# Expert 0's tokens formed by products with strided columns of the token rows, in three parts

## The chip, the cores and the metric

The kernel runs on one core of a Trainium2 chip. The metric is the device time of one execution in microseconds (us). Engines are named as in the profile: PE (TensorE matmul), PEld (its weight loads), DVE (VectorE), ACT (ScalarE), POOL (GpSimd), SP (SyncE, which issues all the DMAs).

## What is computed

One decoder layer on 256 tokens of 1024 features, in float32. A token mixer comes first (gated DeltaNet, a short convolution and cross-attention, each projected, gated and summed, and then an output projection), followed by a residual and a LayerNorm. Then comes the expert part, which is where the change lies:

```
h = layer_norm(DEEPNORM_ALPHA * h + mix)
logits = h @ w_router + b_router             # 32 experts, each token takes its best 4
# for each expert e, over the tokens routed to it:
gate, up = split(x_e @ w_gate_up[e] + b_gate_up[e])         # 1024 -> 2 x 1024
hid = (clip(up, -7, 7) + 1) * min(gate, 7) * sigmoid(1.702 * min(gate, 7))
y_e = (hid @ w_down[e] + b_down[e]) * weight                # 1024 -> 1024
h = layer_norm(DEEPNORM_ALPHA * h + sum over experts of y_e)
```

The weights of one expert are 12 MB, and all 32 are read: this is nearly all of the 453 MB that the kernel moves.

## The kernel before

**The stages.** The mixer runs for the first quarter of the span, by a schedule made in `mixer_schedule` (L100); its products are three float32r products for one float32 product (`three`, L1287). Its last product is `wo`, in two column halves; the second runs from 305.7 to 317 us. Then come the router's logits (L1366), the choice of the four best experts (`top_four`, L1736), and the ranks of the tokens within their expert (schedule step `("rank", 0)`, PE at L1467). After that, 32 items follow, one for each expert. One item takes a block of up to 64 tokens.

**An item on PE.** `gate_up` (L1505) adds the bias by four small products with a one-hot row of the expert (`bias`, L1498), then runs four parts q = 0 to 3. Each part uses one 2 MB piece of weights (two 128-row slices of the 1024 features) against `x_slotT`, the item's tokens with features on partitions (`128x4x128`: four feature blocks, two column halves c of 64 slots). `down` (L1612) uses two more 2 MB pieces. Products with an output of 64 partitions are made in pairs on the two column halves of the array.

**How an item's tokens are made.** Before, in every item: PE gathers the rows by a one-hot product (`gather`, L1484, tokens on partitions), ACT copies them from PSUM to `x_tok` (`copy_rows`, L1235), PE turns four blocks of every fourth column (`turn_tokens`, L1492, columns `slice(b, 4 * P, 4)`, L349), and DVE applies the LayerNorm's gain and bias on the way to `x_slotT` (`copy_tokens`, L1988). For items 1 onward this happens one item ahead, behind the products. For item 0 it stands between the rank step and the first product with weights; `first_tokens` (L2015) does the DVE part in two halves, so that q = 0 waits for `half_tokens` and q = 1 for `tokens_in`.

**The residuals.** The old rows `hx`, scaled by ACT (`scaled_rows`, L1107), are turned back into four PSUM banks by `residual` (L1359), in the order `AGAIN` (L884). One of the four stands behind item 0's gather and the others behind q = 1, 2, 3.

**The ring of weights.** There are 12 places of 2 MB, two items' worth. Piece m goes to place m mod 12 (`ring_place`, L856), and the SP program issues its DMA when the piece that stood there is used (`chunk_spent`, L868): after q = 0, 1, 2 by the semaphore `chunks_used`, after q = 3 by `gu_done`, after the first half of `down` by `chunks_used`, and after the second by `down_done`. Pieces 0 to 5 are item 0's, 6 to 11 item 1's, and 12 is the first whose place item 0 must clear. The places of pieces 0 to 11 overlap what the mixer holds. Piece 2 waits for the mixer's last piece of weights to be split (L938). Pieces 7, 9 and 11 wait for the end of `wo` (L947); place 7 lies exactly over `act_hi` and `act_lo`, the input of `wo`.

**The order of work on PE around the change**, written out at L1659 to L1668: wait for the rank bank to be free, wait for `onehots`, gather, one residual, turn, `gate_up` of item 0, turn of the hidden rows, turn of item 1's tokens, `down`. In the `rank` step, PE turns old rows (`turn_again`, L1353) and then waits for the second mask (L1476).

Of the kernel before, what the change touches and what calls it, by code (L numbers as in the profile page):

```python
# [33 lines left out]
ALU = mybir.AluOpType  # L34
# [3 lines left out]
P = 128  # L38
# [134 lines left out]
def hybrid_layer(nc, x, mem, ln0_g, ln0_b, w_in, conv_qkv, conv_mix, a_log, dt_bias, gdn_norm,  # L173
                 w_mem_kv, w_br, w_o, ln1_g, ln1_b, w_router, b_router, w_gate_up, b_gate_up,
                 w_down, b_down, ln2_g, ln2_b, out):
    with ExitStack() as ctx:
# [147 lines left out]
        wr_o = scratch_o  # L324
        gwr = l.at(x1_o + 512, KD, NE)
        assert l.used >= x1_o + 1536

        def xT(t, k, n=1):

            o = (x1_o + 1024 + k * P if k < 4 else x1_o + (k - 4) * P) if t == 0 else scratch_o + 2 * (1024 - 128) - (KD - k) * P  # L330
            return l.at(o, n * P)
# [48 lines left out]
        bank_free = [sem(f"bank_free{n}") for n in range(BANKS)]  # L380
        bank_hi = sem("bank_hi")
        router_sums, router_row, gains_in = sem("router_sums"), sem("router_row"), sem("gains_in")
        ln1_rows, tokens_made = sem("ln1_rows"), sem("tokens_made")
        again, cut_rows = sem("again"), sem("cut_rows")
        counted, row_made, half_tokens = sem("counted"), sem("row_made"), sem("half_tokens")
        consts, pads = sem("consts"), sem("pads")
# [503 lines left out]
        def _(sp):  # L890
            def bcast(dst, src, done):
                sp.dma_start(dst, src).then_inc(done, 16)

            sp.dma_start(mem_tok, mem[0].rearrange("(t p) d -> p t d", p=P)).then_inc(mem_in, 16)
            slot_dma(sp, 0, 0)
# [41 lines left out]
            for c in range(RAW):  # L937
                raw_spent(sp, N_MIX - RAW + (c - N_MIX) % RAW)  # L938
                chunk_dma(sp, c, w_gate_up[0, 0], w_down[0, 0], *ring_place(c)[0:2])
                if c == 0:  # L940

                    sp.wait_ge(bank_full[bank_of(("br", 0, KD - 1))], turn_of(("br", 0, KD - 1)))
                    for m in BEHIND_BRANCHES:
                        if m == EC:
                            wait_sums(sp, KD)
                        chunk_dma(sp, m - EC, w_gate_up[0, 1], w_down[0, 1], *ring_place(m)[0:2])
            sp.wait_ge(bank_full[bank_of(("wo", 1, 1))], turn_of(("wo", 1, 1)))  # L947
            for m in range(EC, RING):
                if m != SPARE and m not in BEHIND_BRANCHES:
                    chunk_dma(sp, m - EC, w_gate_up[0, 1], w_down[0, 1], *ring_place(m)[0:2])  # L950
# [39 lines left out]
        def _(pool):  # L990
# [90 lines left out]
            eng.memset(ranks, NOT_HERE)  # L1081
            eng.memset(weights, 0.0)
            eng.memset(ids, 0.0).then_inc(moe_consts, 1)


        @block.scalar
        def _(act):
# [147 lines left out]
            def copy_rows(i):  # L1235
                act.wait_ge(gathered, i + 1)
                a.copy(x_tok, ps[0][:, :]).then_inc(rows_copied, 1)  # L1237
# [12 lines left out]

            copy_rows(0)
            for t in range(NT):
# [24 lines left out]
        def _(pe):  # L1277
# [88 lines left out]
            def logit_rows(t, ks):  # L1366
# [17 lines left out]
            for s in SCHEDULE:  # L1384
# [99 lines left out]
            def gather():  # L1484
# [5 lines left out]
                ins.then_inc(gathered, 1)  # L1490

            def turn_tokens(i):  # L1492
                pe.wait_ge(rows_copied, i + 1)
# [4 lines left out]
            def bias():  # L1498

                for c in range(2):  # L1500
                    for n in range(2):
                        rows = slice(NE * (2 * n + c), NE * (2 * n + c + 1))
                        mm(ps[1 + n][64 * c:64 * c + 64, :], e_row[rows, :], bgu[rows, :], start=True, stop=False)  # L1503

            def gate_up(i, places, first=False, tables=False, parts=None):  # L1505

                if first:
                    pe.wait_ge(row_made, 1)
                    pe.wait_ge(ebias_in, 128)
                else:  # L1510
                    pe.wait_ge(tokens_in, i + 1)
                bias()
# [98 lines left out]

            def down(i, places, parts=None, own_scatter=False):  # L1612
                pe.wait_ge(hid_copied, i + 1)
                for q in range(2):
# [43 lines left out]

            pe.wait_ge(bank_free[bank_of(("rank", 0))], turn_of(("rank", 0)))  # L1659
            pe.wait_ge(onehots, 1)  # L1660
# [7 lines left out]
            down(0, item_places(0))  # L1668

            def item(i, places, tables=False, parts=None, own_scatter=False):  # L1670
# [33 lines left out]
        def _(v):  # L1704
# [283 lines left out]
            def copy_tokens(i):  # L1988
                v.wait_ge(x_turned, i + 1)
# [24 lines left out]

            def first_tokens():  # L2015
                v.wait_ge(x_turned, 1)
                slots = x_slotT.rearrange("p b (c n) -> p b c n", c=2)
                rows = ps[0][:, :].rearrange("p (b c n) -> p b c n", b=4, c=2)
                for b, cut, done in ((slice(0, 2), dve_chain, half_tokens), (slice(2, 4), tokens_cut, tokens_in)):
                    ins = d.tensor_tensor(slots[:, b], rows[:, b], over_slots(0)[:, b], ALU.mult)  # L2020
                    if cut is dve_chain:
                        step(ins)
                    else:
                        ins.then_inc(tokens_cut, 1)
                        v.wait_ge(tokens_cut, 1)
                    d.tensor_tensor(slots[:, b], slots[:, b], over_slots(1)[:, b], ALU.add).then_inc(done, 1)
# [11 lines left out]
            v.wait_ge(counted, 1)  # L2038
            step(d.tensor_copy(cnt[0:NE, :], ps[3][0:NE, 0:1]))
            step(d.tensor_scalar(ext[0:NE, :], cnt[0:NE, :], float(CAP), None, ALU.is_gt))  # L2040
# [104 lines left out]
```

## Time and profile before

| | us |
|---|---|
| median of 3 runs (1240.11 to 1240.77) | 1240.73 |
| the profiled execution, its own time | 1240.12 |
| its span, first to last instruction | 1238.4 |
| PE busy | 1209.7 (98%) |
| DVE busy | 388.9 (31%) |
| ACT busy | 252.3 (20%) |
| POOL busy | 152.0 (12%) |

The profiled execution took 1.7 us more than its span (start and end of the program). A row of a timeline gives a start, a duration and the instruction. A float32 product appears as two records (two passes), a transpose as one. A matmul's end is modelled, so the distance between starts tells more than a duration. A row of the chain view gives a start, a duration that belongs to the chain, and the engine and line. A row of the windows view gives a stretch, then the busy time of PE, PEld, DVE, ACT and POOL in it, the granted clock, the DMA engines' mean busy share and GB/s.

### The profile page before, as it was taken

What the parts mean: (1) busy time and instruction counts of PE and PEld (TensorE: products, weight loads), DVE (VectorE), ACT (ScalarE), POOL (GpSimd) and SP (SyncE); (2) the same over time, 40 slices, a digit from 0 to 9 for tenths busy, and PEclk for the clock granted to TensorE, in tenths of its full rate; (3) what the DMA queues carried; (4) which work ended last, traced back from release to release, by engine and by line L of the source; (5) the groups of instructions that cost most, each with busy time, mean ns of one, the idle gap of its engine ahead of it and who ended that gap; (6) DMA issues with size and microseconds to landing.
All of it is one profiled execution on the core that took longest, in us unless ns stands there. A gap on an engine that the chain in (4) does not pass through costs nothing.

```text
span 1238.4 us, 17191 instructions
## 1 busy us (share of the span) xinstructions
PE 1209.7 (98%) x7101; PEld 606.7 (49%) x7101; DVE 388.9 (31%) x780; ACT 252.3 (20%) x420; POOL 152.0 (12%) x108
## 2 busy tenths in 40 slices
PE   9999999999999999999999999999999999999998
PEld 8999999998633333333333333333333333333332
DVE  6575633434622222222222222222222222222223
ACT  4764354544500000000000000000000000000001
POOL 7454323556100000000000000000000000000000
PEclk9999999999999999999999999999999999999999
DMA  9544231879899999999999999999999999999995
GB/s 333 211 153 156 72 136 69 322 293 341 340 429 428 427 429 427 429 429 428 429 428 429 429 427 429 428 429 429 427 429 427 428 429 425 428 428 427 429 421 239
DMA packets 54252, 453.45 MB, mean 366 GB/s; under 512 B 7021, under 2 KB 7098, under 8 KB 29370
## 3 DMA queue, kind: packets, MB, share of 16 engines
q1 hardware_dynamic: 54202, 452.71, 88.2%
q8 instruction: 40, 0.66, 0.2%
q14 instruction: 10, 0.08, 0.0%
HBM read 451.64 MB, written 1.05 MB: 366 GB/s over the span
## 4 chain that ended last, share of the span: by engine, by line
PE 79%; SPq 7%; DMA 6%; DVE 3%; ACT 3%; issue 1%; POOL 0%; DVEq 0%; ACTq 0%; POOLq 0%
PE bank L1524 30%; PE bank L1626 15%; PE bank L1288 6%; PE bank L1289 5%; PE bank L1290 5%; DMA late<-in_w_gate_up_dram 4%; PE bank L1488 4%; PE bank L1648 4%; SPq L832 4%; PE bank L1503 2%; DMA late<-in_w_down_dram 2%; PE bank L1609 2%; SPq L841 1%; ACT late L1247 1%; ACT w_hi L1134 1%
## 5 line engine op out<-in xcount | busy, mean ns | idle before, releaser
L1524 PE MATMUL bank<-late 128*64 128x512 f32 x1536 | 343.1, 595 | 3.6 <-DMA late<-in_w_gate_up_dram 3.6
L1626 PE MATMUL bank<-late 128*64 128x512 f32 x1024 | 229.1, 599 | 6.2 <-ACT late L1247 6.0
L1524 PEld LDWEIGHTS bank<-late 128*64 128x64 f32 x1536 | 107.0, 137 | 220.0 <-issue 210.5
L1626 PEld LDWEIGHTS bank<-late 128*64 128x64 f32 x1024 | 70.8, 137 | 140.9 <-issue 127.2
L1288 PE MATMUL bank<-act_hi,w_hi 128*128 128x256 f32 x448 | 129.5, 289 | 2.1 <-DVE early L1875 1.7
L1289 PE MATMUL bank<-act_lo,w_hi 128*128 128x256 f32 x448 | 125.9, 281 | 0.0
L1290 PE MATMUL bank<-act_hi,w_lo 128*128 128x256 f32 x448 | 125.8, 281 | 0.0
L1998 DVE TENSOR_SCALAR late<-bank 128x512 f32<-128x512 f32 x32 | 22.1, 692 | 304.8 <-PE bank L1524 304.8
L1524 PE MATMUL bank<-raw,late 128*64 128x512 f32 x512 | 116.7, 598 | 0.6 <-DMA raw<-in_w_gate_up_dram 0.6
L795 POOL TENSOR_TENSOR w_lo<-raw,w_hi 128x1024 fp32r<-128x1024 f32 x34 | 84.5, 2486 | 95.8 <-ACT w_hi L1134 95.6
L1288 PEld LDWEIGHTS bank<-act_hi,w_hi 128*128 128x128 f32 x448 | 84.4, 188 | 4.4 <-DVE early L1875 2.3
L1289 PEld LDWEIGHTS bank<-act_lo,w_hi 128*128 128x128 f32 x448 | 84.5, 189 | 0.1
L1290 PEld LDWEIGHTS bank<-act_hi,w_lo 128*128 128x128 f32 x448 | 84.5, 189 | 0.0
L1237 ACT COPY late<-bank 128x512 f32<-128x512 f32 x33 | 19.3, 585 | 303.4 <-PE bank L1488 303.4
L2009 DVE COPY late<-bank 64x512 f32<-64x512 f32 x32 | 22.2, 694 | 184.4 <-PE bank L1626 184.4
L1134 ACT CAST w_hi<-raw 128x1024 fp32r<-128x1024 f32 x56 | 58.7, 1048 | 79.3 <-issue 50.0
L1524 PEld LDWEIGHTS bank<-raw,late 128*64 128x64 f32 x512 | 34.0, 136 | 71.6 <-issue 68.9
L1249 ACT COPY late<-bank 64x512 f32<-64x512 f32 x32 | 18.5, 578 | 233.1 <-PE bank L1626 233.1
L1648 PE MATMUL bank<-late 64*128 64x512 f32 x256 | 63.6, 615 | 0.8 <-DVE late L2009 0.8
L1488 PE MATMUL bank<-hx,late 128*64 128x512 f32 x264 | 62.4, 593 | 0.7 <-DVE late L1975 0.7
L1243 ACT ACTIVATE late<-late 128x512 f32<-128x512 f32 x32 | 20.1, 630 | 187.6 <-DVE late L1998 187.6
L2013 DVE COPY late<-bank 128x256 f32<-128x256 f32 x32 | 13.6, 425 | 119.7 <-PE bank L1643 114.1
(341 smaller groups left out, 1185.6 us busy)
## 6 DMA issues: line engine op xcount, KB each, us to landing
late<-in_w_gate_up_dram SPq DMA_DIRECT2D x94, 2048.0 KB, 34.9
late<-in_w_down_dram SPq DMA_DIRECT2D x62, 2048.0 KB, 34.2
raw<-in_w_gate_up_dram SPq DMA_DIRECT2D x32, 2048.0 KB, 33.8
raw<-in_w_in_dram SPq DMA_DIRECT2D x8, 2048.0 KB, 8.6
early<-in_w_in_dram SPq DMA_DIRECT2D x6, 2048.0 KB, 8.4
raw<-in_w_br_dram SPq DMA_DIRECT2D x3, 2048.0 KB, 7.7
raw<-in_w_mem_kv_dram SPq DMA_DIRECT2D x8, 512.0 KB, 11.2
late<-in_w_down_dram SPq DMA_DIRECT2D x4, 1024.0 KB, 24.4
```

The source lines that it names most:

```text
L795: ops.tensor_tensor(lo, src, as_f32(hi), ALU.subtract).then_inc(split_lo[who], 1)
L832: sp.dma_start(dst, src).then_inc(landed, 16)
L1134: a.copy(hi, src).then_inc(split_hi, 1)
L1288: mm(o, l_hi, r_hi, start=start, stop=False)
L1289: mm(o, l_hi, r_lo, start=False, stop=False)
L1290: return mm(o, l_lo, r_hi, start=False, stop=stop)
L1488: ins = mm(ps[0][64 * c:64 * c + 64, :], onehot[:, t, :], hx[:, t, 512 * c:512 * (c + 1)], start=(t == 0), stop=(t == NT - 1))
L1503: mm(ps[1 + n][64 * c:64 * c + 64, :], e_row[rows, :], bgu[rows, :], start=True, stop=False)
L1524: ins = mm(bk[64 * c:64 * c + 64, :], x_slotT[:, k % 4, 64 * (k // 4):64 * (k // 4) + 64], w[:, kk, at + 512 * c:at + 512 * (c + 1)], star ...
L1609: ins = tr(ps[3][:, c * P:(c + 1) * P], h_tok[:, c:4 * P:4], ident[:])
L1626: ins = mm(ps[3][64 * c:64 * c + 64, :], hidT[:, kk, 64 * q:64 * q + 64], w[:, kk, c * 512:(c + 1) * 512], start=(q == 0 and kk == 0), sto ...
L1648: ins = mm(ps[4 + 2 * t + c][:, :], scatter[64 * c:64 * c + 64, t * P:(t + 1) * P], y_tok[64 * c:64 * c + 64, :], start=False, stop=True, ...
```

## The change

Item 0's tokens are no longer gathered, copied and turned. `tokens_of` multiplies strided columns of the rows `hx` (128 tokens x 128 features, every fourth column, as the stationary operand) with the one-hots (128 x 64), for each of 8 feature blocks and both token tiles: 16 products in three parts (4, 4 and 8). The first two parts stand before q = 0, the third after it. DVE applies gain and bias for each part; q = 0 waits for the first, q = 1 for the second, q = 2 for the third.

The bias products are split: those for the gate's bank stand in the rank step, those for the up bank behind the rank bank's release. The one-hot row of expert 0 is made by POOL and not by DVE. The copy of the counts moves ahead of the first part on DVE. The residuals stand behind q = 0, 1, 2 and behind the first half of `down`. Piece 7 is loaded in two halves of 1 MB, the first as soon as `wo`'s second column half no longer needs the feature slices 0 to 3. Two small buffers change places (`gwr` and half of `xT`), so that `x_slotT` can be written before the first residual is turned.

```diff
-        gwr = l.at(x1_o + 512, KD, NE)
+        gwr = l.at(x1_o, KD, NE)
-            o = (x1_o + 1024 + k * P if k < 4 else x1_o + (k - 4) * P) if t == 0 else ...
+            o = (x1_o + 1024 + k * P if k < 4 else x1_o + 512 + (k - 4) * P) if t == 0 else ...
...
+            def half_chunk(n, landed):
+                src = w_gate_up[0, 1][0:4 * P, :].rearrange("(p k) n -> p k n", k=4)[:, 2:4, :]
+                src = src.rearrange("p k (h n) -> p k h n", n=PIECE)[:, :, n, :]
+                dst = ring_place(EC + 1)[0].rearrange("p (k h n) -> p k h n", k=2, n=PIECE)[:, :, n, :]
+                sp.dma_start(dst, src).then_inc(landed, 16)
...
+            sp.wait_ge(*piece_end[4 * N_MIX - 3])
+            half_chunk(0, half_in)
             sp.wait_ge(bank_full[bank_of(("wo", 1, 1))], turn_of(("wo", 1, 1)))
+            half_chunk(1, ring_place(EC + 1)[1])
             for m in range(EC, RING):
-                if m != SPARE and m not in BEHIND_BRANCHES:
+                if m not in (SPARE, EC + 1) and m not in BEHIND_BRANCHES:
...
             eng.memset(weights, 0.0)
+            eng.tensor_scalar(e_row, part_iota[:, 0:CAP], 0.0, None, ALU.is_equal)
...
-            copy_rows(0)
...
+            def bias(n):
+                for c in range(2):
+                    rows = slice(NE * (2 * n + c), NE * (2 * n + c + 1))
+                    mm(ps[1 + n][64 * c:64 * c + 64, :], e_row[rows, :], bgu[rows, :], start=True, stop=False)
...
                     turn_again(1, 0)
+                    pe.wait_ge(ebias_in, 128)
+                    pe.wait_ge(bank_free[bank_of(("logits", 1))], turn_of(("logits", 1)))
+                    bias(0)
                     pe.wait_ge(r_mask, 2)
...
+            def tokens_of(k0, k1, bk):
+                for k in range(k0, k1):
+                    c, b = k // 4, k % 4
+                    for t in range(NT):
+                        ins = mm(bk[:, b * P + 64 * c:b * P + 64 * c + 64], hx[:, t, 512 * c + b:512 * c + 512:4], onehot[:, t, :],
+                                 start=(t == 0), stop=(t == NT - 1), skip_group_check=True)
+                ins.then_inc(slots_made, 1)
...
                 for q in range(4):
-                    if first and q == 0:
-                        pe.wait_ge(half_tokens, 1)
-                    if first and q == 1:
+                    if first and q < 2:
+                        pe.wait_ge(half_tokens, q + 1)
+                    if first and q == 2:
                         pe.wait_ge(tokens_in, 1)
...
-                    if q > 0 and first:
+                    if q == 0 and first:
+                        tokens_of(4, 8, ps[0])
+                    if q < 3 and first:
                         residual(*AGAIN[q])
...
+                    if first and q == 0:
+                        residual(*AGAIN[3])
...
             pe.wait_ge(bank_free[bank_of(("rank", 0))], turn_of(("rank", 0)))
+            bias(1)
             pe.wait_ge(onehots, 1)
-            gather()
-            residual(0, 1)
-            turn_tokens(0)
+            tokens_of(0, 2, ps[0])
+            pe.wait_ge(counts_read, 1)
+            tokens_of(2, 4, ps[3])
             gate_up(0, item_places(0), first=True)
...
+            pe.wait_ge(half_in, 16)
             item(1, item_places(1))
...
             one_hots(0)
+            v.wait_ge(counted, 1)
+            d.tensor_copy(cnt[0:NE, :], ps[3][0:NE, 0:1]).then_inc(counts_read, 1)
+            v.wait_ge(lnp_in[1], 64)
+            first_tokens(0)
+            first_tokens(1)
             step(d.tensor_copy(ids[:, 0:NE], e_iota))
-            expert_row(0).then_inc(row_made, 1)
-            v.wait_ge(lnp_in[1], 64)
-            first_tokens()
+            first_tokens(2)
```

## Rows read from the trace of the kernel before

**Rows 1.** The page: DMA in 40 slices of the span.
```profile
DMA  9544231879899999999999999999999999999995
GB/s 333 211 153 156 72 136 69 322 293 341 340 429 428 427 429 427 429 429 428 429 428 429 429 427 429 428 429 429 427 429 427 428 429 425 428 428 427 429 421 239
```

**Rows 2.** Windows around the last waits of the mixer and through the experts.
```profile
318.50:320.00 1.50, 1.50 (x14) 1.50 (x15) 1.43 (x5) 0.69 (x2) 0.00 (x0) 1.00 0.61 218
333.40:336.00 2.60, 2.60 (x16) 0.88 (x14) 1.38 (x8) 2.58 (x6) 0.00 (x0) 1.00 0.03 13
336.00:337.50 1.50, 1.50 (x10) 0.43 (x6) 0.00 (x0) 0.13 (x1) 0.00 (x0) 1.00 0.89 186
345.00:1222.00 877.00, 864.24 (x4120) 296.38 (x4118) 202.28 (x424) 75.53 (x127) 0.00 (x0) 1.00 1.01 427
```

**Rows 3.** PE's waits from 1100 to 1225 us: total, times, longest.
```profile
PE bank L1524 <- DMA late<-in_w_gate_up_dram: 3.6, 4, 1.0
```

**Rows 4.** The chain of work from the one-hots to item 2.
```profile
326.53 0.43 DVE late L1975 x2
327.09 1.95 PE bank L1488 x8
330.45 1.02 PE bank L1503 x8
331.50 7.09 PE bank L1524 x32
338.59 0.59 PE bank L1363 x4
349.38 0.68 PE bank L1609 x4
350.82 7.02 PE bank L1626 x32
357.83 1.02 PE bank L1503 x8
...
385.36 1.02 PE bank L1503 x8
```

**Rows 5.** SP's DMA issues: pieces 2, 12 with 13, 16, 17.
```profile
311.59 0.33 SPq L832 DMA_DIRECT2D late<-in_w_gate_up_dram  x1
335.35 3.75 SPq L832 DMA_DIRECT2D raw<-in_w_gate_up_dram  x2
354.58 0.33 SPq L832 DMA_DIRECT2D late<-in_w_down_dram  x1
358.01 0.33 SPq L832 DMA_DIRECT2D late<-in_w_down_dram  x1
```

**Rows 6.** PE's timeline, narrow stretches: products and transposes with a 128x128 stationary operand.
```profile
319.42 3.66 PE L1374 MATMUL bank<-late 128*128 128x32 f32 x32
328.96 0.33 PE L1363 MATMUL bank<-ident,late 128*128 128x128 f32 x1
328.96 0.55 PE L1363 MATMUL bank<-ident,late 128*128 128x128 f32 x3
329.70 0.39 PE L1495 MATMUL bank<-ident,late 128*128 128x128 f32 x1
329.70 0.63 PE L1495 MATMUL bank<-ident,late 128*128 128x128 f32 x3
```

**Rows 7.** Weight loads of such an operand, by line: duration ns min/median/max.
```profile
L1363 PEld LDWEIGHTS bank<-ident,late x16: 138/140/143, 329.0 to 347.1; 128*128 128x128 f32 x16
L1495 PEld LDWEIGHTS bank<-ident,late x132: 195/209/218, 329.7 to 1216.8; 128*128 128x128 f32 x132
```

**Rows 8.** DVE on 128x128, and PE and POOL where the edits with cover stand.
```profile
L1980 DVE TENSOR_SCALAR late<-late x64: 336/340/346, 334.0 to 1198.9; 128x128 f32<-128x128 f32 x64
325.76 0.41 PE L1477 MATMUL bank<-late,before 128*128 128x32 f32 x2 [0.49 <-DVE late L1743]
313.63 0.14 POOL L1083 MEMSET tiny<- 128x49 f32 x1
```

More of the change, by code:

```diff
@@ L324, in hybrid_layer @@
         wr_o = scratch_o
-        gwr = l.at(x1_o + 512, KD, NE)
+        gwr = l.at(x1_o, KD, NE)
         assert l.used >= x1_o + 1536
         def xT(t, k, n=1):
-            o = (x1_o + 1024 + k * P if k < 4 else x1_o + (k - 4) * P) if t == 0 else scratch_o + 2 * (1024 - 128) - (KD - k) * P
+            o = (x1_o + 1024 + k * P if k < 4 else x1_o + 512 + (k - 4) * P) if t == 0 else scratch_o + 2 * (1024 - 128) - (KD - k) * P
             return l.at(o, n * P)
@@ L381, in hybrid_layer @@
         bank_hi = sem("bank_hi")
+        half_in = sem("half_in")
         router_sums, router_row, gains_in = sem("router_sums"), sem("router_row"), sem("gains_in")
@@ L384, in hybrid_layer @@
         again, cut_rows = sem("again"), sem("cut_rows")
-        counted, row_made, half_tokens = sem("counted"), sem("row_made"), sem("half_tokens")
+        counted, counts_read = sem("counted"), sem("counts_read")
+        half_tokens, slots_made = sem("half_tokens"), sem("slots_made")
         consts, pads = sem("consts"), sem("pads")
@@ L1235, in copy_rows @@
             def copy_rows(i):
-                act.wait_ge(gathered, i + 1)
+                act.wait_ge(gathered, i)
                 a.copy(x_tok, ps[0][:, :]).then_inc(rows_copied, 1)
@@ L1490, in gather @@
                 ins.then_inc(gathered, 1)
+            def tokens_of(k0, k1, bk):
[5 more added lines that the diff above has]
+                ins.then_inc(slots_made, 1)
             def turn_tokens(i):
-                pe.wait_ge(rows_copied, i + 1)
+                pe.wait_ge(rows_copied, i)
                 for b in range(4):
@@ L1496, in turn_tokens @@
                 ins.then_inc(x_turned, 1)
[L1498 to L1503, printed above, removed]
             def gate_up(i, places, first=False, tables=False, parts=None):
[L1507 to L1510, printed above, removed]
+                if not first:
                     pe.wait_ge(tokens_in, i + 1)
-                bias()
+                    bias(0)
+                    bias(1)
                 for q in range(4):
-                    if first and q == 0:
-                        pe.wait_ge(half_tokens, 1)
-                    if first and q == 1:
+                    if first and q < 2:
+                        pe.wait_ge(half_tokens, q + 1)
+                    if first and q == 2:
                         pe.wait_ge(tokens_in, 1)
@@ L1610, in turn_hidden, with down @@
                 ins.then_inc(hid_turned, 1)
-            def down(i, places, parts=None, own_scatter=False):
+            def down(i, places, parts=None, own_scatter=False, first=False):
                 pe.wait_ge(hid_copied, i + 1)
@@ L1659, in _ @@
             pe.wait_ge(bank_free[bank_of(("rank", 0))], turn_of(("rank", 0)))
+            bias(1)
             pe.wait_ge(onehots, 1)
-            gather()
-            residual(0, 1)
-            turn_tokens(0)
+            tokens_of(0, 2, ps[0])
+            pe.wait_ge(counts_read, 1)
+            tokens_of(2, 4, ps[3])
             gate_up(0, item_places(0), first=True)
@@ L1667, in _ @@
             turn_tokens(1)
-            down(0, item_places(0))
+            down(0, item_places(0), first=True)
             def item(i, places, tables=False, parts=None, own_scatter=False):
@@ L1988, in copy_tokens @@
             def copy_tokens(i):
-                v.wait_ge(x_turned, i + 1)
+                v.wait_ge(x_turned, i)
                 slots = x_slotT.rearrange("p b (c n) -> p b c n", c=2)
@@ L2013, in copy_scatter, with first_tokens @@
                 d.tensor_copy(scatter, bank[:, 0:T]).then_inc(sc_copied, 1)
-            def first_tokens():
-                v.wait_ge(x_turned, 1)
+            def first_tokens(piece):
+                v.wait_ge(slots_made, piece + 1)
                 slots = x_slotT.rearrange("p b (c n) -> p b c n", c=2)
[L2018 to L2026, printed above, removed]
-            one_hots(0)
+                rows = ps[3 if piece == 1 else 0][:, :].rearrange("p (b c n) -> p b c n", b=4, c=2)
+                b, c = ((slice(0, 2), 0), (slice(2, 4), 0), (slice(0, 4), 1))[piece]
+                ins = d.tensor_tensor(slots[:, b, c], rows[:, b, c], over_slots(0)[:, b, c], ALU.mult)
+                if piece < 2:
+                    step(ins)
+                else:
+                    ins.then_inc(tokens_cut, 1)
+                    v.wait_ge(tokens_cut, 1)
+                d.tensor_tensor(slots[:, b, c], slots[:, b, c], over_slots(1)[:, b, c],
+                                ALU.add).then_inc(half_tokens if piece < 2 else tokens_in, 1)
+            one_hots(0)
+            v.wait_ge(counted, 1)
[3 more added lines that the diff above has]
+            first_tokens(1)
             step(d.tensor_copy(ids[:, 0:NE], e_iota))
-            expert_row(0).then_inc(row_made, 1)
-            v.wait_ge(lnp_in[1], 64)
-            first_tokens()
+            first_tokens(2)
             v.wait_ge(r_exp, 2)
@@ L2037, in _ @@
                                             in1=mask[:, u, :], op0=ALU.mult, op1=ALU.mult))
-            v.wait_ge(counted, 1)
-            step(d.tensor_copy(cnt[0:NE, :], ps[3][0:NE, 0:1]))
+            v.wait_ge(counts_read, 1)
             step(d.tensor_scalar(ext[0:NE, :], cnt[0:NE, :], float(CAP), None, ALU.is_gt))
```

## Prediction

> **What bounds the kernel.** I read the page first. PE is busy for 98% of the span, but the 40 slices show a second resource: from about 341 us to near the end it moves 427 to 429 GB/s in nearly every slice, and no slice is above that [rows 1]. A window over 345 to 1222 us gives 427 GB/s at a share of 1.01 [rows 2]. Two resources look full, so the next view is who waits for whom at the end. PE waits four times for weights of gate and up, 3.6 us in all [rows 3]. The DMA queue itself has no hole after 337 us. So the end is set by the stream of weights: **the moment from which DMA runs without a hole, plus a fixed amount of bytes**. PE arrives late by less than it later waits away.
>
> Where was the last hole? In the windows, 333.4 to 336 us moves 13 GB/s, and 336 to 337.5 only 186 [rows 2]. The ring was full and its data had landed; the next DMA is piece 12, issued at 335.35 us, when item 0's q = 0 has been used [rows 5]. So the start of the unbroken stream hangs on PE's first part of item 0. That is the stretch that the change works on. The chain there is: one-hots until 326.96 us, gather from 327.09, copy and turn, the bias from 330.45, then q = 0 at 331.50 [rows 4].
>
> **From issue to full flow.** In 336 to 337.5 us the 186 GB/s are 0.65 us of full flow, so full flow counts from 336.85 us, 1.5 us after the issue [rows 2, 5]. A 2 MB piece (2.097 MB) at 427 GB/s takes 4.91 us. Before, pieces 12 to 15 last until 336.85 + 4 x 4.91 = 356.49 us. Piece 16 was issued at 354.58 and could flow from 356.08 [rows 5]: in time by 0.4 us, and no more. It waits for the first half of `down`. So the earlier q = 0 is not the whole story; **the gain is what piece 16 permits.**
>
> **The change part by part.** Added: 16 products with a 128x128 stationary operand and 64 moving columns, two passes each, 32 weight loads. The trace has no such product with strided columns. The nearest unstrided one is L1374, 32 passes in 3.66 us, 0.114 us each: with so few columns the loads set the pace. What the stride costs I take from transposes. Three records with stride 4 span 0.63 us and one 0.39, so 0.12 us each once going; unstrided, 0.55 and 0.33, so 0.11 [rows 6]. Scaled, 0.114 x 0.12 / 0.11 = 0.125 us a load, and about 0.1 us once for the first of a run (0.39 less 0.33, and as much for the change of operand). Bounds: 0.11 us, if the stride hides in a two-pass product; 0.209 us, if the strided load's whole duration counts and nothing overlaps [rows 7]. I take 0.125 since it rests on distances between starts.
> The row shows that a stride costs something. The Trainium skill (TensorE: Matmul & The Clock Gate, LDWEIGHTS) lets a load's time go with its column count alone, 107 ns for 128 columns by its formula; by that, an estimate, the 32 loads would take 3.4 us and the end would come some 0.6 us earlier than I say. Against the change speaks SBUF — State Buffer (Door 1: The DMA port swizzle), by which each read that crosses to a new 16-byte line pays a penalty, as every one of these columns does; the page gives no size, and the trace shows 0.01 us a transpose.
>
> Ahead of q = 0: the up bank's bias takes half of L1503's 1.02 us, 0.51, from the rank bank's release, just before the one-hots start at 326.53, so about 326.50, to 327.01; the one-hots end at 326.96 [rows 4]. So it costs 0.05. Then 16 loads: 16 x 0.125 + 0.1 = 2.1 us, to 329.16. Removed is all that stood from 327.09 to 331.50: gather, copy, turn and the bias. DVE's two instructions on the first part are 128x128, 0.34 each [rows 8]: the part is done at 327.06 + 1.1 + 0.15 = 328.3, so DVE ends at about 329.0, hidden by the second part with 0.15 to spare. q = 0 starts at 329.15, not 331.50: **-2.35 us**. Piece 12 is issued at 333.0.
>
> Behind q = 0: the third part, 2.1 us, and a residual, 0.59, which stood behind q = 1 before. q = 1 starts at 329.15 + 3.55 + 2.1 + 0.59 = 335.39, against 335.05 (331.50 and half of 7.09): **+0.34**. Pieces 13, 14 and 15 are issued 0.34 later; 13, the second of a row that ends at 339.10 after 0.33, at 338.76 + 0.34 = 339.1 [rows 5]. Behind q = 3 no residual now stands ahead of the gather, so the turn of the hidden rows comes at 349.38 + 0.34 - 0.59 = 349.13 and `down` at 350.57: -0.25. Piece 16 is issued at 354.33. The fourth residual, in `down`, makes piece 17 and all of item 1 +0.34 (358.35).
>
> DMA: piece 12 flows from 333.0 + 1.5 = 334.5, to 339.41. Piece 13 flows from 339.1 + 1.5 = 340.6: a **new hole of 1.2 us**. Then 14 and 15 follow, to 355.33. Piece 16 can flow from 354.33 + 1.5 = 355.83, a hole of 0.5. Piece 17 needs 360.74 and has 359.85; from item 1 on, PE's 27.5 us an item [rows 4] beat DMA's 6 x 4.91 = 29.5, so no further hole. The stream from piece 16 on starts at 355.83 and not 356.49: **-0.66 us**, and the end with it.
>
> Edits costed at nothing. The gate's bias (0.51) stands where PE idled 0.49 us for the second mask [rows 8], and the turns before it issue their last some 0.2 us earlier; uncovered it would cost 0.1 at most. POOL's one-hot row comes after 313.77 us [rows 8] and is wanted at 321; uncovered, 0.6. The counts' copy on DVE, 0.15, falls in the wait for the first part; `first_tokens(2)` and the table work behind it have 8 us until item 1's gather needs one-hots. ACT loses a copy and comes to its exponentials and the last residual rows earlier. Piece 7's first half is issued behind piece 2, at about 312 us: SP is then free, and the waits behind it are for a later event. It fills 0.7 us of flow that 318.5 to 320 lacked at 218 GB/s [rows 2]; but the queue runs dry before piece 12 in any case, so that hole only grows. It is worth 0.7 only if piece 12 came before 331.2.
>
> **Against the clock.** The profiled execution took 1240.12 us, so the sum gives 1239.46; the median, 1240.73, is 0.61 above it, and 1240.73 - 0.66 = 1240.1.
>
> **Rivals.**
> A, *the early release counts in full*: DMA never starves again after piece 12, since waiting descriptors cover the gap before 13. Then the end moves by 2.35 us, to 1238.4. For it: 333.4 to 336 is the deepest hole. Against: piece 13 can't be issued before its place is clear, and the sum puts that 1.2 us too late.
> B, *slow strided loads* (the other side): place, the 32 loads ahead of piece 16; price, 32 x (p - 0.125) us at a pace p. The gain is gone at p = 0.146. At 0.209 the cost is 2.7, the end +2.0: 1242.8. To lose 2.5 us it takes p = 0.224, above the row's whole duration [rows 7]. For it: a strided load lasts 0.209 us against 0.140 unstrided [rows 7]. Against: records followed each other at 0.12.
> C, *nothing moves at the end*: PE and DMA meet near the end, and PE, 0.34 late from item 1, finishes the tail as before or 0.3 later: 1240.7 to 1241.1. For: PE waits for weights only 3.6 us in all [rows 3]. Against: 0.34 is far below 3.6.
>
> **How the numbers follow.** Forecast 0.62, A 0.08, B 0.17, C 0.13. A measurement of this kernel tells 0.2%, 2.5 us, from no change. The forecast, C and most of B lie within; of A about a third could go beyond with luck in the latencies (0.03), of B a fifth (0.03). The range: the forecast with bounds of 0.11 us (32 x 0.015 = 0.48 earlier, 1239.6) and A's middle below, 1238.8; above, C and two thirds of the way to B's 1242.8: 1241.9. Same 0.94.
>
> **What would show it.** Right: q = 0 starts near 329.2 and SP issues piece 12 near 333.0; a hole in DMA's GB/s near 339.5 to 340.5; the strided product's passes 0.12 to 0.13 us apart; piece 16 issued near 354.3; PE's waits at the end still there. The half piece shows as full flow in 318.5 to 320. Wrong: passes 0.15 us apart or more, `down` of item 0 later than 350.8, the stream whole from piece 12, or an end that moves without piece 16.

## The result, and the profile after

The changed kernel takes 1249.38 us (median of 4, 1248.03 to 1249.53) against 1240.75 for the kernel before on the same chip: ratio 1.0061, interval 1.0044 to 1.0077. It is 8.6 us slower, where 0.7 us faster was forecast and the range ended at 1241.9. The profiled execution took 1249.53 us with a span of 1247.8, so the span grew by 9.4 us.

The page first: DMA in 40 slices. The full rate of about 428 GB/s begins one slice later than in [rows 1], and slices 10 and 11, counted from 0 (312 to 374 us), moved 304 and 357 GB/s in place of 340 and 429.

```profile
PEclk9999999999899999999999999999999999999999
DMA  9644231978799999999999999999999999999995
GB/s 334 214 155 145 80 125 68 350 287 330 304 357 428 428 428 428 429 429 429 429 429 429 428 429 429 429 429 429 429 429 426 428 428 428 427 428 428 428 423 233
```

There is a new row to look at, the granted clock: 8 tenths in slice 10. Before, this row held 9 in all slices. Windows of the changed kernel (PE, PEld, DVE, ACT, POOL busy, granted clock, DMA share, GB/s):

```profile
318.00:323.00 5.00, 4.63 (x42) 4.57 (x42) 4.35 (x18) 3.79 (x6) 0.00 (x0) 1.00 0.99 408
323.00:327.00 4.00, 4.00 (x23) 3.59 (x23) 2.36 (x12) 3.39 (x9) 0.00 (x0) 0.57 1.08 457
327.00:330.00 3.00, 2.84 (x16) 1.16 (x13) 0.76 (x5) 2.99 (x11) 0.00 (x0) 1.00 1.00 415
330.00:337.00 7.00, 7.00 (x25) 4.42 (x27) 1.26 (x5) 2.96 (x6) 0.00 (x0) 0.52 0.40 171
334.00:340.50 6.50, 6.50 (x24) 2.90 (x20) 0.27 (x2) 0.00 (x0) 0.00 (x0) 0.77 0.16 35
345.00:348.00 3.00, 3.00 (x18) 1.08 (x16) 1.17 (x6) 0.00 (x0) 0.00 (x0) 1.00 0.31 98
372.00:1222.00 850.00, 836.32 (x3984) 285.68 (x3982) 191.48 (x404) 72.02 (x121) 0.00 (x0) 1.00 1.01 428
```

Two things stand there. TensorE ran at the lower of its two levels, 1.2 GHz, in most of 323 to 327 and 330 to 337 us. And DMA has a hole of 6.5 us (35 GB/s), where [rows 2] had 2.6 us, and a second one ahead of piece 13. From 372 us on the stream is whole again at 428 GB/s. So the 9 us were lost ahead of that, and the rest of the kernel only carries them. The chain of the same stretch, to be set beside [rows 4]:

```profile
326.78 1.03 PE bank L1394 x4
327.81 0.35 PE bank L1499 x2
328.19 0.30 DVE late L1990 x2
328.53 1.07 PE bank L1394 x4
329.60 3.93 PE bank L1519 x16
333.53 5.34 PE bank L1546 x16
338.87 3.88 PE bank L1519 x16
342.75 0.45 PE bank L1376 x4
343.19 3.58 PE bank L1546 x16
```

L1394 is the split bias, L1519 the strided products, L1546 the products with weights. Each pair of bias products takes 1.03 or 1.07 us, not 0.51. Each eight strided products (16 passes) take 3.9 us, not 2.1. And q = 0 takes 5.34 us, not 3.55. SP's issues of pieces 12, 13, 16 and 17, beside [rows 5]:

```profile
339.07 0.35 SPq L834 DMA_DIRECT2D raw<-in_w_gate_up_dram  x1
346.95 0.34 SPq L834 DMA_DIRECT2D raw<-in_w_gate_up_dram  x1
362.25 0.33 SPq L834 DMA_DIRECT2D late<-in_w_down_dram  x1
366.42 0.33 SPq L834 DMA_DIRECT2D late<-in_w_down_dram  x1
```

Piece 12 is 3.7 us later than before, piece 13 8.2, piece 16 7.7 and piece 17 8.4 us.

### The profile page after: what moved, and what is told of

Its sections match the earlier page's. It is cut to its first block, busy times and chain, and to the rows that moved or that the text cites. A ratio compares the mean times of both kernels' runs of the same rounds, so it can differ in the third digit from the quotient of the medians.

```text
span 1247.8 us, 17204 instructions
## 1 busy us (share of the span) xinstructions
PE 1218.6 (98%) x7121; PEld 613.9 (49%) x7121; DVE 388.7 (31%) x781; ACT 252.0 (20%) x419; POOL 152.5 (12%) x109
## 4 chain that ended last, share of the span: by engine, by line
PE 81%; DMA 8%; ACT 3%; DVE 3%; SPq 2%; issue 1%; POOL 0%; another core or an unknown queue 0%; ACTq 0%; DVEq 0%
PE bank L1546 31%; PE bank L1650 16%; DMA late<-in_w_gate_up_dram 8%; PE bank L1301 6%; PE bank L1302 5%; PE bank L1303 5%; PE bank L1674 4%; PE bank L1510 4%; PE bank L1394 2%; SPq L834 2%; PE bank L1633 2%; ACT late L1261 1%; ACT w_hi L1148 1%; PE bank L1669 1%; PE bank L1519 1%
## 5 line engine op out<-in xcount | busy, mean ns | idle before, releaser
L1546 PE MATMUL bank<-late 128*64 128x512 f32 x1536 | 343.3, 595 | 4.1 <-DMA late<-in_w_gate_up_dram 4.1
L1546 PEld LDWEIGHTS bank<-late 128*64 128x64 f32 x1536 | 106.7, 137 | 221.1 <-issue 209.8
L1546 PE MATMUL bank<-raw,late 128*64 128x512 f32 x512 | 118.7, 606 | 1.2 <-DMA raw<-in_w_gate_up_dram 1.2
L1546 PEld LDWEIGHTS bank<-raw,late 128*64 128x64 f32 x512 | 34.3, 138 | 72.4 <-issue 69.1
```

Source lines behind the costliest of these rows:

```text
L1546: ins = mm(bk[64 * c:64 * c + 64, :], x_slotT[:, k % 4, 64 * (k // 4):64 * (k // 4) + 64], w[:, kk, at + 512 * c:at + 512 * (c + 1)], star ...
```

## The experiments

Four questions were open: what the stride costs, what the split bias costs, what the low clock costs and whether the change brings it, and whether the end really follows the start of the unbroken stream. All medians are over the executions given in brackets; ratios are to the kernel before on the same chip. The first four experiments stood beside 1240.72 for the kernel before (25), the next four beside 1241.37 (19), the last four beside 1240.83 (25).

**Neighbouring columns in place of strided ones** (expert 0's tokens then hold other features than its weights' rows; the work is the same).

```diff
-  hx[:, t, 512 * c + b:512 * c + 512:4], onehot[:, t, :],
+  hx[:, t, P * k:P * (k + 1)], onehot[:, t, :],
```

> The changed kernel, but the 16 products that form expert 0's tokens read 128 neighbouring columns instead of every fourth (the work is the same, expert 0's tokens hold the wrong features). Theory S (the stride makes each weight load take 0.24 us, at either clock): the 32 loads come down to about 0.11 us each, 4 us less of PE ahead of piece 16, and the time falls by 3 to 4.5 us, to 1245 to 1246.5. Theory K (the low clock from 323 us on is the larger part): the loads stay near 0.2 us while the clock is low, and the time falls by less than 1.5 us. If the clock stays high here, both together: 1240 to 1241.

Measured: 1244.49 us (10; 1240.90 to 1249.61), ratio 1.0030 (1.0015 to 1.0045): 4.9 us less than the changed kernel. The executions differ in their clock (1.000 at 1240.9, 0.992 at 1249.6), so this difference mixes stride and clock; the price of the stride is read from the timeline. PE's timeline of the profiled execution (1241.77 us), which had the high clock throughout this stretch:

```profile
325.11 1.07 PE L1394 MATMUL bank<-late 32*64 32x512 f32 x4
326.11 0.41 PE L1499 MATMUL bank<-late,before 128*128 128x32 f32 x2
326.90 1.07 PE L1394 MATMUL bank<-late 32*64 32x512 f32 x4 [0.16 <-DVE late L1990]
327.90 2.00 PE L1519 MATMUL bank<-late,hx 128*128 128x64 f32 x16
329.83 3.65 PE L1546 MATMUL bank<-raw,late 128*64 128x512 f32 x16
```

Sixteen passes take 1.93 us from start to start, 0.12 each: the stride alone makes 0.12 into 0.24 us. The two bias rows show the second mis-sized term at the high clock: the second mask's product starts at 326.11, against 325.76 [rows 8], and the first strided product at 327.90, where 327.06 was forecast.
This kernel also shows a third thing. Piece 16 was issued at 354.92 us, only 0.34 later than before, and from 312 to 355 us both kernels moved 376 GB/s. Yet the stream then lost more than 0.34. Windows over 355 to 363 us, first of the kernel before, then of this one:

```profile
355.00:363.00 8.00, 8.00 (x42) 2.38 (x40) 1.27 (x4) 0.58 (x1) 0.00 (x0) 1.00 1.00 424
```

```profile
355.00:363.00 8.00, 8.00 (x44) 2.42 (x41) 1.11 (x3) 0.58 (x1) 0.00 (x0) 1.00 0.96 373
```

8 us at 373 in place of 424 GB/s are 8 x 51 / 427 = 1.0 us of flow. By the prediction's arithmetic (a piece flows 1.5 us after its issue at the earliest, and for 4.91 us) nothing would be lost: with piece 12 issued at 333.69 and 13 at 339.62, the queue is empty from 355.85, piece 16 flows from 356.42, and the kernel before has 356.49. So where the queue runs dry more than once, as it does here ahead of pieces 13 and 16, that arithmetic says too little.

**The half piece alone**, in the kernel before.

```diff
+            sp.wait_ge(*piece_end[4 * N_MIX - 3])
+            half_chunk(0, half_in)
             sp.wait_ge(bank_full[bank_of(("wo", 1, 1))], turn_of(("wo", 1, 1)))
+            half_chunk(1, ring_place(EC + 1)[1])
...
-                if m != SPARE and m not in BEHIND_BRANCHES:
+                if m not in (SPARE, EC + 1) and m not in BEHIND_BRANCHES:
...
+            pe.wait_ge(half_in, 16)
```

> The kernel before with nothing but piece 7 loaded in two halves. Theory that the end follows piece 12 and piece 16: within 0.3 us of before (1240.4 to 1241.1), with a longer hole ahead of piece 12. If two 1 MB DMAs with 4 KB rows are slower or disturb the queue: 1 us or more above. If this is what lets the clock fall at 323 us: the granted clock falls here too, and the time rises by 2 us or more.

Measured: 1241.38 us (10; 1240.26 to 1243.84), ratio 1.0007 (0.9997 to 1.0016), not told apart from before. Its profiled execution took 1240.29, with the granted clock at 0.999. Piece 12 was issued at 335.31 us, as before, so what the half piece brought forward was given back in the hole.

**The bias moved alone**, in the kernel before, with gather, copy and turn as they were.

```diff
                     turn_again(1, 0)
+                    bias(0)
                     pe.wait_ge(r_mask, 2)
...
+            bias(1)
             pe.wait_ge(onehots, 1)
             gather()
```

> The kernel before with the bias products moved (the gate's into the rank step, the up bank's behind the rank bank) and the one-hot row made by POOL; gather, copy, turn and the order of the residuals as before. By PE's chain q = 0 starts 0 to 0.1 us earlier or later, since DVE ends its first half at 331.45 in any case: 1240.3 to 1241.1 if the clock stays high. Theory K1 (the bias products in the rank step or POOL's step bring the low clock): granted clock 0.995, 2 us or more above. Theory K2 (the low clock comes from the long stretch of 64-column products behind it): clock 0.999 as before.

Measured: 1241.81 us (10; 1241.06 to 1247.24), ratio 1.0018 (1.0005 to 1.0031). The forecast of no cost falls: at the high clock, item 0's products with weights start at 332.35 us, against 331.50 before, and piece 12 is issued at 336.20, 0.85 later. The gather behind the bias starts at 327.90 in place of 327.09, and the rest of the chain, DVE's copy included, follows it.

```profile
326.90 1.07 PE L1382 MATMUL bank<-late 32*64 32x512 f32 x4 [0.16 <-DVE late L1964]
327.90 1.94 PE L1498 MATMUL bank<-hx,late 128*64 128x512 f32 x8
...
332.35 7.09 PE L1525 MATMUL bank<-raw,late 128*64 128x512 f32 x32 [1.08 <-DVE late L2028]
```

The clock was 0.998 in this execution, but two of the ten stood at 0.994 and took 1247.2 us.

**The changed kernel with piece 7 whole.**

```diff
-            half_chunk(0, half_in)
...
-            half_chunk(1, ring_place(EC + 1)[1])
...
-                if m not in (SPARE, EC + 1) and m not in BEHIND_BRANCHES:
+                if m != SPARE and m not in BEHIND_BRANCHES:
...
-            pe.wait_ge(half_in, 16)
```

> The changed kernel with piece 7 loaded whole again. If the half piece is worth nothing, as the prediction says: 1249.4 within 0.5 us. If the halves cause the low clock that begins at 323 us, before PE comes to any changed instruction: the clock stays at 1 until 330 us and the time falls by 2 us or more.

Measured: 1247.86 us (4; 1247.37 to 1248.78), ratio 1.0058 (1.0041 to 1.0075): 1.5 us less than the changed kernel's first measurement, 0.75 less than its second (below). The half piece is not what costs. Here the clock was high until 328 us and then low, and q = 0 is again slow:

```profile
323.00:328.00 5.00, 4.84 (x36) 2.97 (x35) 3.21 (x18) 4.26 (x10) 0.00 (x0) 1.00 0.99 423
328.00:335.00 7.00, 7.00 (x26) 4.81 (x26) 1.26 (x5) 5.07 (x15) 0.00 (x0) 0.53 0.79 337
```

```profile
328.05 4.00 PE L1518 MATMUL bank<-late,hx 128*128 128x64 f32 x16
331.98 5.24 PE L1545 MATMUL bank<-raw,late 128*64 128x512 f32 x16
337.15 3.95 PE L1518 MATMUL bank<-late,hx 128*128 128x64 f32 x16
```

The strided passes take 3.93 us ahead of q = 0 at the low clock, and 3.79 to the next start behind it at the high one (the next starts at 340.94): a strided load is not paced by the clock.

**The bias whole again**, in the changed kernel.

```diff
-                    pe.wait_ge(ebias_in, 128)
-                    pe.wait_ge(bank_free[bank_of(("logits", 1))], turn_of(("logits", 1)))
-                    bias(0)
...
-            bias(1)
+            pe.wait_ge(ebias_in, 128)
+            whole_bias()
             pe.wait_ge(onehots, 1)
```

> The changed kernel with expert 0's four bias products together again, behind the rank bank's release (none in the rank step). Theory B (the four products run side by side on four groups of 32 rows and take about 1.0 us together, and each half of the split pair takes 1.0 us too): the four stand in 1.0 us, the rank step is 0.35 us shorter, q = 0 starts 0.35 us earlier than with the split at the same clock, and the time falls by 0.3 to 0.5 us where the clock is alike. If half the products took half the time, as predicted, this is 0 to 0.1 us later than the changed kernel.

Measured: 1247.48 us (4; 1247.09 to 1248.19), ratio 1.0051 (1.0035 to 1.0068): 1.9 us less than the changed kernel's first measurement, 1.1 less than its second (below), where 0.3 to 0.5 was expected at like clocks. In its profiled execution the granted clock was 1.00 from 326.5 to 340 us, so the bias and both parts of the strided products ran at 2.4 GHz. Then it fell to 1.2, and q = 1 took 5.24 us (340.05 to 345.29) in place of 3.6. The time thus holds another share of the low clock, and the rows tell more than it does. All four products take what one pair took, and 16 strided passes take 3.88 us:

```profile
327.25 1.09 PE L1401 MATMUL bank<-late 32*64 32x512 f32 x8 [0.16 <-DVE late L1995]
328.26 3.94 PE L1523 MATMUL bank<-late,hx 128*128 128x64 f32 x16
332.14 3.65 PE L1550 MATMUL bank<-raw,late 128*64 128x512 f32 x16
```

**Extra products, narrow or wide**, in the kernel before, ahead of item 0's gather. Two kernels: 16 products of 64 columns, or 8 of 512 columns (two more gathers). The first part below is the narrow kernel, the second the wide one; what they write is overwritten.

```diff
+            for k in range(KD):
+                for t in range(NT):
+                    mm(ps[0][:, 64 * k:64 * k + 64], hx[:, t, P * k:P * (k + 1)], onehot[:, t, :], ...)
...
+            for _ in range(2):
+                for t in range(NT):
+                    for c in range(2):
+                        mm(ps[0][64 * c:64 * c + 64, :], onehot[:, t, :], hx[:, t, 512 * c:512 * (c + 1)], ...)
             gather()
```

> The kernel before with 16 extra products (128 neighbouring columns as the stationary operand, 64 moving columns, 32 loads) ahead of item 0's gather, whose results the gather overwrites. As PE work they cost 3.7 us ahead of q = 0 and of piece 16: the end moves by 3.7 us, 1244.4, if the clock stays as in the kernel before (0.998 to 0.999). Theory K2 (a long stretch of narrow products is what brings the low clock): the granted clock is 0.997 or less in most runs, and the time 1 to 5 us above that of the kernel with wide extras.

> The kernel before with two more gathers (8 products of 512 columns, 3.6 us) ahead of item 0's gather: the same PE time as the narrow extras, but wide. Both theories: 3.6 us later, 1244.3. Theory K2: the granted clock stays at 0.998 to 0.999 in nearly all runs, and this kernel's runs lie closer together than those with narrow extras. If the clock is a matter of where the stretch falls and not of the width: both kernels show the same clocks and the same spread.

Measured: narrow 1248.23 us (4; 1247.08 to 1250.26; granted clock 0.993 to 0.996), ratio 1.0053 (1.0036 to 1.0070), 6.9 us for 3.7 of work. Wide 1244.13 us (10; 1243.18 to 1245.74; 0.997 to 0.999), ratio 1.0024 (1.0015 to 1.0034), 2.8 us for 3.6 of work. The same PE time at the high clock, but 4.1 us apart. In both profiled executions the clock fell at 322 to 322.5 us. Then, narrow:

```profile
322.00:328.00 6.00, 5.76 (x33) 5.61 (x32) 3.47 (x20) 3.24 (x9) 0.00 (x0) 0.53 1.01 431
328.00:339.00 11.00, 10.62 (x41) 7.69 (x41) 0.57 (x4) 0.00 (x0) 0.00 (x0) 0.50 0.46 195
```

```profile
328.38 7.06 PE L1663 MATMUL bank<-late,hx 128*128 128x64 f32 x32 [0.62 <-DVE late L1979]
```

and wide:

```profile
322.00:326.00 4.00, 4.00 (x24) 4.00 (x24) 3.07 (x16) 2.44 (x7) 0.00 (x0) 0.57 1.04 446
326.00:340.00 14.00, 13.18 (x74) 5.61 (x74) 5.03 (x23) 7.71 (x20) 0.00 (x0) 1.00 0.50 211
```

```profile
327.71 3.65 PE L1664 MATMUL bank<-hx,late 128*64 128x512 f32 x16 [0.70 <-DVE late L1980]
```

The fall came in both kernels ahead of every extra instruction. In the narrow kernel the clock was still at 1.2 GHz when the extras began, they took 7.0 us in place of about 3.7, and it stayed low until 339 us. In the wide kernel it was back at 2.4 by 326 us, 1.7 us ahead of the first extra product. So this pair of profiles does not show that wide products bring the clock back. What sets the two kernels apart is the granted clock of all executions: 4 of 4 at 0.996 or below with the narrow extras, 10 of 10 at 0.997 or above with the wide ones.

**A kernel built from the results**: neighbouring columns, with expert 0's weights of gate and up loaded to match, as blocks of 128 neighbouring rows; the bias whole; the residuals one place later.

```diff
+                src = w_gate_up[0, 0][2 * P * c:2 * P * (c + 1), :].rearrange("(k p) n -> p k n", p=P)
+                sp.dma_start(dst.rearrange("p (k n) -> p k n", k=2), src).then_inc(landed, 16)
...
-                    if q < 3 and first:
-                        residual(*AGAIN[q])
+                    if q == 1 and first:
+                        residual(*AGAIN[0])
+                    if q == 2 and first:
+                        residual(*AGAIN[1])
+                        residual(*AGAIN[2])
```

> The changed kernel with expert 0's weights of gate and up loaded as blocks of 128 neighbouring rows, so that its tokens are formed with neighbouring columns (gain and bias from the columns kept on partitions), the whole bias together, and the residuals behind q = 1 (one) and q = 2 (two) instead of q = 0, 1, 2. Theory that strided loads and split bias are the mis-sized terms and that the end follows pieces 12, 13 and 16: at the high clock q = 0 starts near 329.0, piece 12 is issued at 332.9, 13 at 338.4, 16 near 353.4, and the time is 1239.3 to 1240.2 where the clock stays high; runs with a low clock lie 2 to 6 us above. Rival (row blocks of 8 KB for the DMA are slower): piece 0 to 3 land later, PE waits for them in item 0.

Measured: 1241.12 us (10; 1240.27 to 1242.94), ratio 0.9997 (0.9987 to 1.0007): 8 us less than the changed kernel, and the same as before. Its profiled execution (1240.66 us, span 1238.9) shows why it isn't faster:

```profile
327.55 2.00 PE L1532 MATMUL bank<-late,hx 128*128 128x64 f32 x16
329.48 3.65 PE L1559 MATMUL bank<-raw,late 128*64 128x512 f32 x16
349.31 0.75 PE L1649 MATMUL bank<-ident,late 128*128 128x128 f32 x4 [0.16 <-DVE late L2050]
```

```profile
333.33 5.83 SPq L834 DMA_DIRECT2D raw<-in_w_gate_up_dram  x2
354.56 4.50 SPq L834 DMA_DIRECT2D late<-in_w_down_dram  x2
```

q = 0 starts 2.0 us earlier than before and so does piece 12. But piece 16 is issued at 354.56, as before (354.58): the turn of the hidden rows now waits for DVE's last step (0.16 us idle ahead of it), and starts at 349.31 in place of 349.38. I expected piece 16 at 353.4 and forgot that chain. There is a second reason. By the prediction's arithmetic the early piece 12 would still be worth 0.4 us: with pieces 12, 13 and 16 issued at 333.33, 338.82 and 354.56, piece 16 flows from 356.06 in place of 356.49. The stream was not earlier but about 0.8 us later (windows below, in the part on the prediction).

**Extra PE work late or early**, in the kernel before: one more gather (its four products, 1.8 us) in item 24; the same ahead of item 0; two more (3.6 us) in item 24.

```diff
+                        if isinstance(i, int) and i == 24:
+                            for t in range(NT):
+                                for c in range(2):
+                                    mm(ps[0][64 * c:64 * c + 64, :], onehot[:, t, :], hx[:, t, 512 * c:512 * (c + 1)],
+                                       start=(t == 0), stop=(t == NT - 1))
                         gather()
```

The early one has the same loop ahead of item 0's `gather()`; the long one has it twice in item 24.

> The kernel before with one more gather (1.8 us of wide products) in item 24. Theory that the end is the stream's: PE meets the stream only from about 1110 us on and has 3.6 us of waits there to give, so 1240.7 within 0.4 us. If PE's own work set the end: 1.8 us later.

> The kernel before with the same extra gather ahead of item 0's. Theory that the end is the stream's and that the stream's start hangs on piece 12: 1.8 us later, 1242.5, at like clocks. If nothing ahead of piece 12 mattered: as before.

> The kernel before with two more gathers (3.6 us) in item 24, to set beside the same two ahead of item 0's, which cost about 3 us. Theory that the end is the stream's: 3.6 us of PE's waits are just used up, so 0 to 0.8 us later. If PE's own work set the end: 3.6 us.

Measured: late and short 1240.89 us (10), ratio 0.9997 (0.9988 to 1.0007); early and short 1242.58 (10), ratio 1.0014 (1.0005 to 1.0024), 1.75 us for 1.8 of work; late and long 1240.44 (10), ratio 1.0001 (0.9992 to 1.0011), nothing for 3.6. In the last, PE's waits for weights near the end shrank from four of 3.6 us in all [rows 3] to

```profile
PE bank L1524 <- DMA late<-in_w_gate_up_dram: 2.0, 2, 1.0
```

The end is the stream's, and its start hangs on PE's work ahead of the first pieces that item 0 releases. The profiled execution of the late and long kernel (1243.99 us, the slowest of its ten) shows one thing more. Up to item 24 it is the kernel before, and yet:

```profile
323.00:330.00 7.00, 6.38 (x33) 5.68 (x34) 3.42 (x18) 2.90 (x8) 0.00 (x0) 0.50 1.02 433
```

So the fall at 322 to 323 us comes with no instruction changed ahead of it. The late and short kernel's profiled execution (1241.00 us) had it too, from 323 to 326 us.

**The changed kernel again.**

> The changed kernel as it is, once more, for more executions at other phases of the clock. Theory that the narrow stretch brings a low clock wherever it falls: every execution is at 0.997 or less and takes 1247 to 1250 us. If the low clock of the first profile was chance: some executions at 0.999, near 1245.

Measured: 1248.61 us (4; 1248.26 to 1249.11), ratio 1.0062 (1.0045 to 1.0079), at a granted clock of 0.995 or 0.996 in every execution. Of 25 executions of the kernel before on that chip, 22 stood at 0.998 or more (1240.05 to 1241.85 us) and 3 at 0.995 (1243.47 to 1243.77).

## Why the prediction was wrong

**The bound was right.** The end follows the start of the unbroken stream, and PE's own time does not set it: 3.6 us of extra products cost nothing late, 1.8 us early cost 1.75. The half piece is worth nothing. This part of the text held; its sums of PE's time, of the clock and of the holes did not.

**The step that failed first: "0.125 us a load".** The range for it was drawn from transposes with stride 4, whose records follow each other at 0.12 against 0.11 us [rows 6]. A float32 product in two passes with strided columns takes 3.93 us for 16 loads, 0.245 each, above even the upper bound of 0.209 that the text took from [rows 7]. 32 loads: 3.93 + 3.88 - 4.2 = +3.6 us. This was rival B, and past its point of 0.224; its chance, 0.17, was too small, and its bound was no bound, since it took the duration of a transpose's load (0.209 us) for that of a product's: the strided product's loads last 0.329 us, and 0.192 with neighbouring columns. That a load's time goes with its column count alone, which the prediction set beside its price, is not so here: both kernels load 128 columns. Against the change the text set the rule of the Trainium skill (SBUF — State Buffer, Door 1: The DMA port swizzle) on reads that cross to a new 16-byte line. The trace agrees that such reads cost more: 0.12 us a load here.

**The second: the split bias, "half of L1503's 1.02 us", and "free in the idle 0.49".** The four products of [rows 4], each on its own group of 32 rows, take 1.0 us together; two of them take 1.0 us too. So the gate's pair outlasts the wait for the mask by 0.35 us, and the up bank's pair costs 0.5 more than forecast: +0.84 at the start of the first strided product, 327.90 for 327.06 (and +0.85 on piece 12 with the bias moved alone).

**The third was not in the text at all: the clock.** The sum was made at 2.4 GHz throughout, since that is what the kernel before had in its one profile. In the changed kernel's, the low stretches cost 1.6 us in the rank step (the first strided product starts at 329.53 us in PE's timeline, against 327.90 with neighbouring columns at the high clock: 1.6 us) and 5.34 - 3.58 = 1.8 us in q = 0.

The sum with these terms: -0.25 (forecast for piece 16) + 3.6 + 0.84 + 1.6 + 1.8 = 7.6, measured 362.25 - 354.58 = 7.7 us.

**The fourth: the arithmetic of the holes**, "piece 16 can flow from 354.33 + 1.5" and "the end with it". It holds where all pieces are late together: with one early extra gather it gives +1.76, and 379 in place of 391 GB/s over 312 to 372 us is 1.7 us. It fails where the queue runs dry more than once. The same window for the kernel before, the one with neighbouring columns, the one built from the results and the changed one:

```profile
312.00:372.00 60.00, 58.32 (x316) 27.80 (x316) 23.32 (x86) 17.28 (x37) 1.58 (x6) 1.00 0.95 391
312.00:372.00 60.00, 59.15 (x330) 29.82 (x330) 23.32 (x87) 16.72 (x36) 1.95 (x7) 1.00 0.96 384
312.00:372.00 60.00, 58.66 (x332) 29.95 (x332) 23.38 (x87) 16.73 (x36) 1.99 (x7) 1.00 0.97 385
312.00:372.00 60.00, 59.16 (x296) 33.19 (x296) 23.18 (x87) 16.13 (x35) 1.98 (x7) 0.91 0.83 326
```

Against the first, the others are behind by 60 x 7 / 427 = 1.0, 0.8 and 9.1 us; the arithmetic says 0.07 ahead, 0.43 ahead and 7.3 behind. So it misses 1.1 to 1.9 us each time, and the gain of 0.66 us was doubtful even with every price of PE right: the kernel built from the results comes close to that case and gained nothing. Why the flow is below full when pieces come one by one into an empty queue was not tried.

The span grew by 9.4, 1.7 more than piece 16. The last landing moved by 8.8, so 1.1 of them are of this fourth kind, and 0.6 stand behind it. There the last wait of the changed kernel's PE for weights ends at 1192.77 us. The same wait ends at 1182.96 in the kernel before, which waits once more, 0.17 us for its last weights at 1223.49. Why the first of them ends 9.8 us later and not 8.8 stays open.

How much of the clock is the change's? The fall at 322 to 323 us need not be: of the six profiled executions with nothing changed ahead of it, four had it (narrow and wide extras, late and short, late and long) and two had not (the kernel before, early and short). A fall behind 326 us is seen only where the tokens are formed with strided columns: from 330 us in both profiles of the changed kernel, from 328 with piece 7 whole, from 340 with the bias whole. Over all executions, the changed kernel stood at 0.996 or below in 8 of 8, the kernel before in 3 of 25 on the same chip, the one with narrow extras in 4 of 4, the one with wide extras in 0 of 10. With neighbouring columns and the split bias it was 5 of 10, from 1240.9 us at a clock of 1.000 to 1249.6 at 0.992. So that narrow products in place of the gather bring more time at 1.2 GHz is supported by these counts; whether it is their width, their stride or the length of the stretch was not varied one by one, and stays open.

Rival A would have needed the pieces behind 12 to come early as well; they came about 8 us late. Rival C's premise was refuted by the late extras. The "new hole ahead of piece 13" was there, 98 GB/s in 345 to 348 us, but further holes followed.

## What to carry to other kernels

A stationary operand with strided columns must be priced as a product of the same kind, not as a transpose: here each load doubled. Where the end is a full stream of DMAs, add up PE's time only as far as the first pieces that it releases, ask which release has the least lead, and look at what waits on the other engines' chain there (DVE's last step set piece 16 once PE was early). Bringing one piece forward while the next stays where it is adds a hole, and each further hole cost more than the gap in the issues: compare the bytes moved over the whole stretch, not the issues alone. A stretch of narrow products costs more than its own time if the stretch behind it runs at 1.2 GHz, and one profiled execution does not show how often that happens: look at the granted clock of all of them. And before a recovery of the clock is put down to an instruction, look whether it came ahead of it.

## What the runs showed of the hardware

- A float32 pass whose 128 stationary columns are 16 bytes apart takes 0.24 us at 2.4 GHz (3.88 us for 16, bias whole) and 0.245 at 1.2 GHz (3.93 for 16, piece 7 whole). With neighbouring columns it is 0.12 at 2.4 and 0.22 at 1.2 (7.0 us for 32 passes in the kernel with narrow extras). So only the plain load goes with the clock.
- A transpose with the same stride is no price for it: its records follow each other at 0.12 us [rows 6].
- Two bias products on 32 rows each take the same 1.0 us as the four that cover all 128 rows.
- The fall to 1.2 GHz at 322 to 323 us comes in some executions of kernels that are the same up to there and not in others. Before it, in the changed kernel, PE was busy for 4.6 us of 5 (318 to 323), mostly with products of 32 columns and transposes.
- With equal bytes moved up to 355 us, a DMA issued 0.34 us later at the point with the least lead, and the one behind it 1.1 us later (359.09 for 358.01), cost the stream 1.0 us.
